# The scores of two half iterations in every second w_in slot of a hybrid decoder step

## What is computed

```python
z = h @ p['w_in']                                   # 23 groups of columns in this kernel
gq, gk, gv, gg, glr, sq, sk, sv, cu = jnp.split(z, offs, axis=-1)
# stick-breaking attention of the 8 sequences, over 2048 cached positions and the new ones
z = jnp.einsum('bqhd,bkhd->bhqk', qblk, kf) * scale + bf
log_1mb = jnp.where(mask, jax.nn.log_sigmoid(-z), 0.0)
tail = lax.cumsum(log_1mb, axis=3, reverse=True) - log_1mb
w = jnp.where(mask, jnp.exp(jax.nn.log_sigmoid(z) + tail), 0.0)
return jnp.einsum('bhqk,bkhd->bqhd', w, vf)
```

## Time and profile before

| | |
|---|---|
| median of 3 runs | 1428.11 us (1423.18 to 1428.42) |
| profiled execution | 1427.58 us, its span 1425.9 us |
| PE busy | 1397.9 us |
| DVE busy | 896.5 us |
| ACT busy | 734.3 us |
| w_in stage, slots 7 to 22, first layer | about 284 to 404 us |

### The profile page before, as it was taken

How to read it: one execution, slowest core, us unless ns; L and a number is a source line. 1 busy time by engine, 2 the same in 40 slices (tenths; PEclk the granted TensorE clock), 3 DMA queues, 4 the chain that set the end, 5 groups by cost and what they waited for, 6 DMA issues and landing times.

```text
span 1425.9 us, 26859 instructions
## 1 busy us (share of the span) xinstructions
PE 1397.9 (98%) x10531; PEld 1322.6 (93%) x10531; DVE 896.5 (63%) x1493; ACT 734.3 (51%) x1195; POOL 182.7 (13%) x333
## 2 busy tenths in 40 slices
PE   7999999999999999999999999999999999999998
PEld 6999999988867999999999999999888689999998
DVE  5665633679984766553467664446899747765542
ACT  4544433588855554443355434445886555543431
POOL 1020000323253020000000000021424410000000
PEclk9999999999999999999999999999999999999999
DMA  9575455577787595545545554565877885554441
GB/s 245 148 208 151 143 153 157 144 213 223 214 280 229 141 271 148 148 140 153 156 129 149 152 152 138 150 168 152 248 211 228 263 249 156 154 150 146 139 146 51
DMA packets 391554, 249.41 MB, mean 175 GB/s; under 512 B 16513, under 2 KB 379638, under 8 KB 391428
## 3 DMA queue, kind: packets, MB, share of 16 engines
q1 hardware_dynamic: 375602, 204.94, 50.5%
q0 software_dynamic: 15520, 42.62, 9.6%
q10 hardware_dynamic: 306, 0.13, 0.0%
HBM read 242.10 MB, written 5.53 MB: 174 GB/s over the span
## 4 chain that ended last, share of the span: by engine, by line
PE 91%; DVE 4%; ACT 3%; issue 1%; DMA 0%; SPq 0%; DVEq 0%; ACTq 0%
PE bank L592 23%; PE bank L594 23%; PE bank L593 23%; PE bank L849 3%; PE bank L959 2%; PE bank L628 2%; PE bank L632 2%; PE bank L629 2%; DVE fT L1744 2%; PE bank L864 2%; PE bank L1035 1%; PE bank L814 1%; PE bank L1074 1%; DVE w_l L1572 1%; PE bank L1076 1%
## 5 line engine op out<-in xcount | busy, mean ns | idle before, releaser
L1572 DVE TENSOR_TENSOR w_l<-raw,w_h 128x1024 fp32r<-128x1024 f32 (+1 forms) x332 | 395.0, 1196 | 293.3 <-ACT w_h L1208 293.3
L592 PE MATMUL bank<-hh,w_h 128*128 128x320 f32 x1632 | 512.5, 314 | 0.0
L594 PE MATMUL bank<-hh,w_l 128*128 128x320 f32 x1632 | 504.3, 309 | 0.0
L593 PE MATMUL bank<-hl,w_h 128*128 128x320 f32 x1632 | 504.2, 309 | 0.0
L1208 ACT ACTIVATE w_h<-raw 128x1024 fp32r<-128x1024 f32 (+1 forms) x332 | 331.8, 1030 | 135.7 <-DMA raw<-in_ffn_w_down 100.3
L592 PEld LDWEIGHTS bank<-hh,w_h 128*128 128x128 f32 x1632 | 306.4, 188 | 10.5 <-issue 8.6
L593 PEld LDWEIGHTS bank<-hl,w_h 128*128 128x128 f32 x1632 | 306.5, 188 | 0.6
L594 PEld LDWEIGHTS bank<-hh,w_l 128*128 128x128 f32 x1632 | 306.3, 188 | 0.0
L592 PE MATMUL bank<-guh,w_h 128*128 128x320 f32 x704 | 217.7, 309 | 0.0
L594 PE MATMUL bank<-guh,w_l 128*128 128x320 f32 x704 | 217.3, 309 | 0.0
L593 PE MATMUL bank<-gul,w_h 128*128 128x320 f32 x704 | 217.3, 309 | 0.0
(11 more groups left out here) (286 smaller groups left out, 1644.3 us busy)
## 6 DMA issues: line engine op xcount, KB each, us to landing
raw<-in_ffn_w_gate SPq DMA_DIRECT2D x88, 512.0 KB, 3.9
raw<-in_ffn_w_up SPq DMA_DIRECT2D x88, 512.0 KB, 3.9
raw<-in_ffn_w_down SPq DMA_DIRECT2D x64, 448.0 KB, 3.7
raw<-in_w_in SPq DMA_DIRECT2D x44, 512.0 KB, 3.9
raw<-in_ffn_w_down SPq DMA_DIRECT2D x32, 512.0 KB, 4.0
kpg<-in_cache_sb_k SPq DMA_DIRECT2D x112, 128.0 KB, 3.3
kpg<-in_cache_sb_k POOLq DMA_DIRECT2D x112, 128.0 KB, 2.6
raw<-in_w_out SPq DMA_DIRECT2D x16, 512.0 KB, 7.3
```

Of the source, the lines that this page charges most:

```text
L592: pe.matmul(out, w_h[:, slot, k, :], rhs_h[:, k0 + k, :], start=first, stop=False)
L593: pe.matmul(out, w_h[:, slot, k, :], rhs_l[:, k0 + k, :], start=False, stop=False)
L594: last = pe.matmul(out, w_l[:, slot, k, :], rhs_h[:, k0 + k, :], start=False, stop=end)
L1572: V(dve.tensor_tensor(w_l[:, slot, 0:n, :], raw[:, slot, 0:n, :], w_h[:, slot, 0:n, :].bitcast(F32), ALU.subtract), sm["w_lo"])
```

## The change

PE no longer computes one half iteration's scores in every slot. At a slot of even h (from 2 to 16) it computes those of h - 2 and of h - 1 behind each other, at the place where only h - 1 stood; at a slot of odd h it computes none. In slots 10 and 12, with two h each, the same rule holds: in slot 10 (3 and 4) both run at the inner place, in slot 12 (6 and 7) both at the start. Nothing else is altered: the same instructions, buffers and waits on every other engine.

```diff
@@ -985,7 +985,8 @@
                     h, last_h = TURNS[m][0], TURNS[m][-1]
                     if h < 2 * ITS:
                         turn_keys(h, (0, 1))
-                    if 0 < h <= 2 * ITS:
+                    if h and h % 2 == 0:
+                        scores(h - 2)
                         scores(h - 1)
                     if m == 8:
                         new_scores()
@@ -1004,7 +1005,9 @@
                         unit(u, out, hh, hl, part=range(3, 5))
                         turn_keys(last_h, (0, 1))
                         unit(u, out, hh, hl, part=range(5, 6))
-                        scores(h)
+                        if last_h % 2 == 0:
+                            scores(last_h - 2)
+                            scores(last_h - 1)
                         unit(u, out, hh, hl, part=range(6, 7))
                     if last_h < 2 * ITS:
                         turn_keys(last_h, (2, 3))
```

## The result

The changed kernel takes 1435.72 us (median of 8 runs, 1434.57 to 1440.06), the kernel before, run beside it, 1428.26 us (8 runs, 1423.18 to 1430.47): ratio 1.0056, 95% interval 1.004 to 1.0071. It is slower by 7.5 us, where the prediction said +1.6 us and held 1424 to 1436 possible: 1435.72 lies just inside that range, whose upper end had been set for another cause (the clock). The profiled execution took 1435.49 us, 7.9 us more than the profiled one of before.

What follows compares the result with a forecast made beforehand. PE is 98% busy, but DVE's unbroken last run was taken to end the w_in stage. Two layers times (0.3 later take-up + 0.5 stall for w_out 1) = +1.6 us: 1429.2 us, range 1424 to 1436.

Steps and rivals of the forecast that it cites:

- PE's saving in a pair: w_in stage: a second S adds 0.86 us, a removed one saves 1.18 or 1.00; about 1.9 us PE time per layer.
- DVE, not PE, ends the stage: End of w_in stage: PE waits 2.00 us for DVE's last scaled unit; DVE's last run has no slack.
- the rival in which it arrives: Whole kernel: DVE gets inputs earlier everywhere, so PE's saving counts: -3.8 us, 1423.8 us; chance 0.10.
- Slot 14: At sample product L829 PE waits for DVE, which cuts off the gain; ACT's chain comes some 0.2 us earlier.
- +0.3 us a layer for the delayed take-up: Slot 19: key copies wait for same-slot scores, so ACT takes scores up later, delaying DVE's last run; bounds -0.3 to +0.9.
- The issue of w_out 1: SyncE's queue: value loads wait for scores 14, now in slot 21; w_out 1 issued at 394.6, 4.7 us later.
- The landing of w_out 1: End of w_in stage: landing 5.3 us after issue, DVE stalling 0.5 us per layer (range 0 to 2.8).
- a late w_out 1: End of w_in stage: w_out 1 lands as slowly as before, +6.2 us in all, 1433.8 us; chance 0.20.
- The clock in slot 11: PE's idle grows from 0.35 to about 1.5 us; a clock fall in both layers costs 6.8, 1436.0 us; chance 0.15 (one or both).
- The half rate at the end of the stage: PE's longer idle before L1084 could make the existing half-clock stretch half as long again, adding 1.7 us a layer.

Runs made afterwards that it cites:

- the kernel with the load in front of the eight: Changed kernel; SyncE issues the load of w_out 1 behind the same wait (scores 14) but before iteration 1's eight value loads: 1428.87 us, ratio 1.0011.
- the kernel before with w_out 1 first: Kernel before, with SyncE's load of w_out 1 placed before the value loads of iteration 1: 1428.83 us, ratio 0.9995.

## Why the prediction was right or wrong

Start-up (0.71 us) is taken off in all comparisons of times here.

- **PE's saving in a pair: right.** In the changed kernel's timeline of PE:

```profile
297.11 1.03 PE L849 MATMUL bank<-const,kpg 128*128 128x128 f32 x8
297.90 0.39 PE L592 MATMUL bank<-hh,w_h 128*128 128x320 f32 x1
...
302.46 1.93 PE L864 MATMUL bank<-kT,qb 128*32 128x256 f32 x32
304.32 0.41 PE L592 MATMUL bank<-hh,w_h 128*128 128x320 f32 x1
```

  Transposes straight to the unit 0.79, a pair of scores to the unit 304.32 - 302.46 = 1.86 = 1.00 + 0.86, as taken.
- **DVE, not PE, ends the stage: right.** None of the saving arrived while the last scaling stood at the end of DVE's run, and the rival in which it arrives (1423.8) fell.
- **Slot 14: off by 0.25.** The sample product started 0.05 us later (335.07 with 0.55 us of wait, before 334.31), not 0.2 earlier. ACT's chain had gained nothing.
- **+0.3 us a layer for the delayed take-up: the mechanism right, the size 0.6.** The rows of PE, ACT and DVE in slot 19, to be read beside the earlier trace rows:

```profile
375.25 1.93 PE L864 MATMUL bank<-kT,qb 128*32 128x256 f32 x32
...
376.45 1.08 ACT L1370 ACTIVATE kT<-bank 128x512 f32<-128x512 f32 x2 [1.52 <-PE bank L864]
377.42 0.69 ACT L1379 ACTIVATE z__106<-bank,bq 128x512 f32<-128x512 f32 x1
...
379.67 1.23 DVE L1575 TENSOR_TENSOR w_l<-raw,w_h 128x1024 fp32r<-128x1024 f32 x1 [1.63 <-ACT w_h L1211]
```

  Take-up 377.42 - 375.25 = 2.17 us behind the first scores (worked out: 2.12). PE came into the slot 375.25 - 374.98 - 0.71 = 0.44 earlier and not 0.66, which is slot 14's quarter of a microsecond. DVE's last run began 379.67 - 378.36 - 0.71 = 0.60 later.
- **The issue of w_out 1: right.** 394.70 against 394.6. Net of start-up it is 4.1 later, since the eight issues took 4.35 us and not 5.24.
- **The landing of w_out 1: here the prediction failed.** I took 5.3 us and a stall of 0.5 a layer, arguing that the traffic would largely be gone. (Even by its own numbers 5.3 us give 394.6 + 5.3 + 1.06 - 400.25 = 0.7.) It landed after 7.84 us (second layer 1105.33 - 1097.87 = 7.46), and DVE stalled 2.39 and 1.73 us; 4.1 in all where the sum had 1.0. Between the profiled executions 7.9 - 1.6 = 6.3 us are missing from the sum, and these 3.1 are the largest piece. The next are the clock at the second FFN, 1.4, start-up, 0.7, the later take-up, 2 x 0.3, and two waits for value loads, 2 x 0.3. Of these only the take-up had a term in the sum. The traffic had not gone, since the eight value loads moved with the load behind them. Windows of the changed kernel (the last two columns are the DMA share and GB/s), then of the kernel before:

```profile
396.00:398.00 2.00, 2.00 (x17) 1.67 (x19) 1.93 (x3) 0.00 (x0) 1.09 (x2) 1.00 0.90 295
398.00:400.00 2.00, 2.00 (x34) 1.07 (x34) 1.93 (x7) 0.00 (x0) 0.00 (x0) 1.00 1.03 323
400.00:402.00 2.00, 2.00 (x16) 1.92 (x14) 1.23 (x5) 0.00 (x0) 1.08 (x2) 1.00 0.86 253
```

```profile
396.00:398.00 2.00, 2.00 (x25) 1.33 (x27) 1.93 (x5) 0.72 (x1) 1.08 (x2) 1.00 0.94 296
398.00:400.00 2.00, 2.00 (x28) 1.42 (x21) 1.96 (x8) 0.68 (x2) 0.28 (x1) 1.00 0.42 129
```

  Before, the DMA engines fell to 0.42 of their time once w_out 1 was there; now they are full until it lands. GpSimd's loads, whose end I had counted on, came only 0.8 earlier, net of start-up (392.23 and 396.44 against 392.32 and 396.52), and GpSimd went on to the next iteration's. About 5.3 us is the landing for another order, that of the kernel with the load in front of the eight, where it took 5.2 (5.9 in the second layer). With this tensor's usual landing the rival "a late w_out 1", 1433.8 us at a chance of 0.20, is what happened; it lacks another 0.3 of take-up per layer and the clock. That the measured time still fell inside 1424 to 1436 is luck: the range reached that far for the clock's fall in slot 11, which did not come.
- **The clock in slot 11: the idle as worked out, the fall not.** PE idled 1.54 us there (worked out: 1.5; 1.55 in the second layer) and the granted clock, last number but two of a window, stayed at 1.00 (timeline, then windows, of the changed kernel):

```profile
310.95 1.12 PE L849 MATMUL bank<-const,kpg 128*128 128x128 f32 x8 [1.54 <-ACT kT L1370]
```

```profile
311.50:312.00 0.50, 0.50 (x6) 0.50 (x6) 0.50 (x2) 0.50 (x1) 0.00 (x0) 1.00 1.03 328
312.50:313.00 0.50, 0.50 (x7) 0.50 (x5) 0.50 (x3) 0.50 (x2) 0.45 (x2) 1.00 0.13 41
```

- **The half rate at the end of the stage: in part.** It begins at about 405.5 and ends at about 412.3, 6.8 us as before, behind an idle of 4.89; in the second layer it lasts 10.2 us, half as long again, as this rival said, behind an idle of 4.23. So the longer idle did not make the longer stretch here.

## What to carry to other kernels

When a wait is released later, shift the whole block of issues behind it, with its traffic: a load at the end of the block then has the same loads ahead of it, and here it took the landing time of before (7.8 us against 7.4) and not the shorter one of a quieter time. Where the one load that a busy engine needs next stands behind bulk loads that are needed much later, put it in front of them; here this alone took back the change's cost as far as the times can tell (ratio 0.9993, interval 0.9974 to 1.0012). And a saving on an engine that isn't the bound can show at most once the release that it waits for is taken from behind the work that doesn't need it; here that, too, took back the loss, and a gain beyond it is not shown.

## What the runs showed of the hardware

The same idle of PE did not always bring the clock down. Behind the stage of the first layer PE idled 2.00 us in the kernel before, and the granted clock fell to 0.50, 1.2 GHz, 1.6 us after PE had stopped. In the kernel before with w_out 1 first, PE idled 2.00 us at the same place and it stayed at 1.00, 2.4 GHz (that kernel's timeline, then its windows):

```profile
405.07 0.50 PE L1087 MATMUL bank<-qs,ks 64*128 64x128 f32 x4 [2.00 <-DVE fT L1800]
```

```profile
404.50:405.00 0.50, 0.00 (x0) 0.00 (x0) 0.50 (x2) 0.00 (x0) 0.45 (x2) 1.00 1.00 332
405.00:405.50 0.50, 0.43 (x6) 0.43 (x8) 0.02 (x1) 0.00 (x0) 0.45 (x2) 1.00 1.07 340
406.00:406.50 0.50, 0.50 (x5) 0.24 (x3) 0.00 (x0) 0.00 (x0) 0.00 (x0) 1.00 0.91 223
```

At the entry of the second FFN an idle of 0.94 us left it at 1.00 in the kernel before; in the changed kernel, with the same 0.94 us, it fell (windows of the changed kernel; the third number from the end is the granted clock):

```profile
483.50:484.00 0.50, 0.15 (x1) 0.15 (x2) 0.47 (x2) 0.50 (x2) 0.00 (x0) 1.00 0.00 0
484.00:484.50 0.50, 0.50 (x3) 0.50 (x4) 0.50 (x2) 0.43 (x2) 0.00 (x0) 0.56 0.00 0
487.50:488.00 0.50, 0.50 (x6) 0.50 (x5) 0.50 (x2) 0.30 (x1) 0.00 (x0) 1.00 0.00 0
```

That stretch cost 1.4 us and belongs to no instruction that the change moved. The profiled execution of the kernel before with w_out 1 first had no such stretch between the first stage and its last few microseconds and took 1424.33 us, at a median of 1428.83 for its kernel. So a few microseconds between single executions here are the clock's, and a difference of that size between two profiles is no finding; the medians of several runs, read with their granted clocks, and the waits in the stage are. All eight runs of the changed kernel have a mean granted clock of 0.988 to 0.995, and those of the kernel before 0.990 to 1.000 with a mean of 0.996. So more time at half clock does come with the late load. Whether the longer idle alone makes it, the runs don't tell.
